# Merged block transfers, units fetched earlier, and head squares moved in a hybrid encoder layer

## The chip, the cores and the metric

One core of one Trainium2 chip runs the whole kernel in one launch. The metric is the device time of an execution in microseconds. TensorE multiplies, VectorE and ScalarE work on tiles, GpSimd masks and gathers, SP only issues transfers, all in program order; they meet at semaphores.

## The reference

One encoder layer over a prompt of 256 tokens and a sample of 1024, together T = 1280 rows of width 1024:

```
xn   = rmsnorm(x, norm1_g)
proj = xn @ w_in                        # pool 512 | q 512 | k 512 | v 512 | o 512 | gates 16
a    = multiscale_pool(proj[pool])      # 4 windows, a 128x128 map for each
m    = sigmoid(o) * head_norm(mlstm_forward(q,k,v) + mlstm_backward(q,k,v)) * head_g
x    = x + concat(a, m) @ w_out
x    = x + hier_moe(rmsnorm(x, norm2_g))   # 32 experts, top 2 in the best group
y    = rmsnorm(x, final_norm_g)
```

The mLSTM has 4 heads of 128 channels and works by chunks of 128 tokens. For a chunk and a direction, with b the running sum of the log forget gates:

```
s    = (q k^T) * exp(logw - m_row)           # logw masked to the direction's triangle
num  = s v + inter * (C q);  den = sum(s) + inter * (n q)
h    = num / max(|den|, exp(-m_row))
C, n = decay * (C, n) + (u * k)^T (v, 1)
```

Then h of both directions is summed, divided by its root mean square per head, and weighted.

## The kernel before

All matrix products with weights are made of three products of a high and a low part (`product3`): `w_hi` is a rounded copy that ScalarE makes, `w_lo` the rest that VectorE makes.

**Projection.** The list `proj` names the input projections, each a slice of 128 output columns by a segment of tokens (512, 512, 256). The last twelve are those of q: four slices of segment 0, four of segment 1, four of segment 2; the last one is NPROJ-1. `w_hi` and `w_lo` hold four slices, `w_st` stages two. A slice m is loaded by `slice_in(m)` on SP, split by `w_part(m)` on ScalarE and VectorE as soon as the slice four before it has been used last. The last four slices, V0 to V3 (NSL-4 to NSL-1), are those of the values; the value projection needs all four and runs over ten token tiles. ScalarE evicts results in `take(n)`, which also splits slices (`parts_after`).

**Blocks.** The parts of the mLSTM that don't depend on the state are made ahead, in 20 blocks of one chunk by two heads (`BLOCKS`): SP loads rows of gate values broadcast to all partitions (`block_in`, two transfers), GpSimd masks, ScalarE takes the exponential (`block_weights`), TensorE transposes keys and makes scores (`block_scores`), VectorE multiplies (`block_products`), SP stores to DRAM (`block_out`, three transfers). Blocks 0 to 7 (N_EARLY) go through three stages beside the last eight q projections, one behind each (`blocks_after`); the others through five stages beside the value projection (`blocks_with`). On SP everything stands in one order: at block i the slices V2 and V3 (i = 4 and 5), then `block_out(i)`, then a `block_in`.

**Scan.** 20 units, a step of one direction each (`unit`): SP loads what the blocks stored (`unit_load`; the first two units into the dead half of `xT_lo`, the others into four slots), TensorE makes numerators and the state's gain (`unit_rows`), VectorE the denominators and the state (`heads_out`), ScalarE evicts h. Beside it the eight slices of w_out come in (`wo_in`) and are split, at each odd unit from 1 to 15. A unit needs the eviction two units before it. As tiles of h are complete in both directions, VectorE sums them (`head_sum`), ScalarE squares them and takes roots (`head_squares`, `head_roots`), VectorE makes the reciprocal, ScalarE scales (`norm_heads`). Six of ten tiles are squared in the scan (EARLY), four behind the first tile of the output projection.

**Output projection.** Ten token tiles (`out_rows`, two halves of 512 columns), each with transposes of h (`h_transposes`), `mix`, its high and low parts, residual, second norm, and the router. Then the expert stage and the final norm.

## Time and profile before

| what | us |
|---|---|
| median of 3 runs | 1243.17 (1243.12 to 1247.94) |
| the profiled execution | 1245.86 |
| its span | 1244.1 |
| TensorE busy | 1115.8 (90%) |
| VectorE busy | 866.1 (70%) |
| ScalarE busy | 683.6 (55%) |
| GpSimd busy | 186.1 (15%) |

Times in the trace are microseconds from the span's start. Projections end at 292, the value projection at 355.8, the scan at 420.2, the output projection at 566; the expert stage takes the rest. Durations of one instruction overlap with those beside it: matmuls are pipelined, so the step from start to start is what counts.

### The profile page before, as it was taken

The numbers are of one execution on the slowest core, as the hardware profiler recorded it, in microseconds if no ns is written. First come the engines' busy times: TensorE is split into PE (matmuls) and PEld (weight loads), VectorE is DVE, ScalarE is ACT, GpSimd is POOL, SyncE is SP. The second block draws the span as 40 slices with busy tenths as digits, with TensorE's granted clock in tenths as the row PEclk, the third lists the DMA queues.
The fourth block names the chain that finished last, engine by engine and source line by source line (L and its number), as shares of the span: only waits on it lengthen the run. The fifth ranks groups of instructions, "written<-read, shape, count | busy, mean of one in ns | idle before, by whom it ended". The sixth has DMA issues, their size and how long they took to land.

```text
span 1244.1 us, 17907 instructions
## 1 busy us (share of the span) xinstructions
PE 1115.8 (90%) x5679; PEld 936.1 (75%) x5679; DVE 866.1 (70%) x1334; ACT 683.6 (55%) x1122; POOL 186.1 (15%) x285
## 2 busy tenths in 40 slices
PE   5999999998988899992799999999999999999910
PEld 4888888887877788882688888888888888888810
DVE  5649510135345566656589999999999999999958
ACT  5432231234346633313577777877877787787633
POOL 1100210001200012223012212211211221221100
PEclk9999999999999999996799999999999999999965
DMA  8212240448988335445889999999999999999667
GB/s 233 60 32 80 89 124 1 120 132 252 298 283 307 134 135 158 148 170 195 282 290 362 384 379 384 370 388 385 380 388 386 384 381 389 376 383 382 251 244 301
DMA packets 161137, 324.04 MB, mean 260 GB/s; under 512 B 24577, under 2 KB 91649, under 8 KB 161089
## 3 DMA queue, kind: packets, MB, share of 16 engines
q1 hardware_dynamic: 145184, 281.81, 63.5%
q0 software_dynamic: 15904, 41.61, 8.7%
q8 instruction: 28, 0.46, 0.1%
q14 instruction: 21, 0.16, 0.0%
HBM read 285.35 MB, written 51.11 MB: 270 GB/s over the span
## 4 chain that ended last, share of the span: by engine, by line
PE 75%; DVE 10%; DMA 5%; ACT 5%; issue 3%; SPq 1%; POOL 1%; ACTq 0%; POOLq 0%; DVEq 0%
PE psum L805 23%; PE psum L807 22%; PE psum L806 22%; DVE e_lo L1718 3%; ACT e_hi L1280 3%; PE psum L1018 2%; PE psum L975 1%; PE psum L1051 1%; DMA w_st<-in_w_out_dram 1%; DVE x L1828 1%; DVE x L1836 1%; DVE x L1826 1%; PE psum L963 1%; PE psum L841 1%; DMA gx<-xn_scratch,rows_to 1%
## 5 line engine op out<-in xcount | busy, mean ns | idle before, releaser
L1718 DVE TENSOR_TENSOR e_lo<-e_st,e_hi 128x1024 fp32r<-128x1024 f32 x384 | 442.6, 1222 | 16.8 <-ACT e_hi L1280 16.0
L1280 ACT ACTIVATE e_hi<-e_st 128x1024 fp32r<-128x1024 f32 x384 | 372.1, 1050 | 10.7 <-PE psum L807 9.8
L805 PE MATMUL psum<-e_hi,ex_hi 128*128 128x512 f32 x512 | 204.8, 400 | 8.6 <-DVE ex_lo L1759 3.7
L806 PE MATMUL psum<-e_lo,ex_hi 128*128 128x512 f32 x512 | 201.3, 393 | 0.0
L807 PE MATMUL psum<-e_hi,ex_lo 128*128 128x512 f32 x512 | 201.1, 393 | 0.0
L805 PE MATMUL psum<-xT_hi,w_hi 128*128 128x512 f32 (+1 forms) x408 | 147.3, 361 | 4.5 <-DVE xT_lo L1399 3.0
L807 PE MATMUL psum<-xT_hi,w_lo 128*128 128x512 f32 (+1 forms) x408 | 145.6, 357 | 0.0
L806 PE MATMUL psum<-xT_lo,w_hi 128*128 128x512 f32 (+1 forms) x408 | 145.5, 357 | 0.0
L805 PEld LDWEIGHTS psum<-e_hi,ex_hi 128*128 128x128 f32 x512 | 96.8, 189 | 41.5 <-DVE e_lo L1718 16.2
L807 PEld LDWEIGHTS psum<-e_hi,ex_lo 128*128 128x128 f32 x512 | 97.0, 189 | 20.9
L806 PEld LDWEIGHTS psum<-e_lo,ex_hi 128*128 128x128 f32 x512 | 97.1, 190 | 19.2
L805 PE MATMUL psum<-e_hi,ht_hi 128*128 128x512 f32 x256 | 105.9, 414 | 1.3 <-DVE yo L1771 1.1
L807 PE MATMUL psum<-e_hi,ht_lo 128*128 128x512 f32 x256 | 100.5, 393 | 0.0
L806 PE MATMUL psum<-e_lo,ht_hi 128*128 128x512 f32 x256 | 100.1, 391 | 0.0
L772 POOL COPY row_to<-rows_to 128x1 int32 (+1 forms) x32 | 28.8, 899 | 417.1 <-DVE yo L1771 417.1
L805 PEld LDWEIGHTS psum<-xT_hi,w_hi 128*128 128x128 f32 x408 | 77.9, 191 | 15.7 <-issue 3.4
L807 PEld LDWEIGHTS psum<-xT_hi,w_lo 128*128 128x128 f32 x408 | 77.8, 191 | 11.0
L1391 DVE TENSOR_TENSOR w_lo<-w_st,w_hi 128x1024 fp32r<-128x1024 f32 x21 | 25.6, 1223 | 86.7 <-ACT w_hi L1088 86.6
L806 PEld LDWEIGHTS psum<-xT_lo,w_hi 128*128 128x128 f32 x408 | 77.8, 191 | 10.7
L805 PE MATMUL psum<-wo_hi,mix_hi 128*128 128x512 f32 x160 | 64.9, 405 | 1.9 <-DVE mix_lo L1624 1.9
L806 PE MATMUL psum<-wo_lo,mix_hi 128*128 128x512 f32 x160 | 63.2, 395 | 0.0
L807 PE MATMUL psum<-wo_hi,mix_lo 128*128 128x512 f32 x160 | 63.1, 394 | 0.0
(226 smaller groups left out, 1717.0 us busy)
## 6 DMA issues: line engine op xcount, KB each, us to landing
e_st<-in_expert_w_gate_dram SPq DMA_DIRECT2D x128, 512.0 KB, 5.6
e_st<-in_expert_w_up_dram SPq DMA_DIRECT2D x128, 512.0 KB, 6.2
e_st<-in_expert_w_down_dram SPq DMA_DIRECT2D x128, 512.0 KB, 8.5
w_st<-in_w_in_dram SPq DMA_DIRECT2D x20, 512.0 KB, 4.2
xn_scratch<-xn POOLq DMA_DIRECT2D x20, 512.0 KB, 3.8
f_y<-expert_rows SPq DMA_DIRECT2D x20, 512.0 KB, 12.2
units<-mlstm_units SPq DMA_DIRECT2D x18, 512.0 KB, 5.4
b_wgt<-gate_rows SPq DMA_DIRECT2D x20, 256.0 KB, 4.5
```

Source lines behind the costliest of these rows:

```text
L772: pool.tensor_copy(row_to[:, b:b + 1], rows_to[:, bass.ds(i, 1)]).then_inc(row_placed, 1)
L805: pe.matmul(out, a_hi, b_hi, start=start, stop=False)
L806: pe.matmul(out, a_hi, b_lo, start=False, stop=False)
L807: return pe.matmul(out, a_lo, b_hi, start=False, stop=stop)
L841: last = pe.matmul(out[:, col:col + m], wpool[:, g, :], u_ext[:, g, first:first + m], start=True, stop=True)
L963: last = pe.transpose(psum[:, 5 + k // 4, (k % 4) * P:(k % 4 + 1) * P], x1[:, order[t], k:D:KD], ident[:, :])
L975: last = pe.matmul(psum[:, 7, 0:NL], x1T[:, k, :], rw[:, k, :], start=(k == 0), stop=(k == KD - 1))
L1018: last = pe.transpose(psum[:, 2 + k // 4, (k % 4) * P:(k % 4 + 1) * P], gx[:, b, k:D:KD], ident[:, :])
L1051: last = pe.transpose(psum[:, 6, k * P:(k + 1) * P], hh[:, k:F:KF], ident[:, :])
L1280: act.activation(e_hi[:, r, :, :], e_st[:, slot, :, :], ACT.Copy).then_inc(ehi_done, 1)
L1391: dve.tensor_tensor(w_lo[:, m % 4, :, :], w_st[:, m % 2, :, :], w_hi[:, m % 4, :, :].bitcast(F32), ALU.subtract).then_inc(wlo_done, 1)
L1718: dve.tensor_tensor(e_lo[:, r, :, :], e_st[:, slot, :, :], e_hi[:, r, :, :].bitcast(F32), ALU.subtract).then_inc(elo_done, 1)
```

## The change

- A block's rows (`rows_dram`), its stage in SBUF and its result in DRAM (`units_dram`) are each laid out in the order weights forward, inter forward, weights back, inter back, keys back. One load and one store do for a block; stage 4 is split over two places and keeps two of each. `back_keys_dram` is gone.
- The blocks 0 and 1 come after the projections NQ+2 and NQ+3 of segment 0, where NQ is now the first q projection, 2 to 5 after those of segment 1, 6 and 7 after NPROJ-3 and NPROJ-1. Blocks 0 and 1 wait for the evictions of the queries of their heads.
- SP issues V2 and V3 at block 7, ahead of `block_out(7)` and behind `block_out(6)`.
- Four units (N_FAR) go to the dead half of `xT_lo`: 0, 1 and 2 are loaded at blocks 11, 13 and 15, unit 3 after the last value projection. A later unit is one transfer in either direction.
- The slices of w_out are split at units 4, 5, 7, 9, 11, 13, 15 and 16 (`wo_at`).
- In the scan ScalarE squares tiles 0 and 1 after units 6 and 8, takes their roots after 10, scales them after 12 and 14, and squares tile 2 after 16; tile 3 follows the scan, and tiles 4 to 9 are squared one at a time in the output projection, with a reciprocal for each. The first tile's transposes, `mix` and `mix_hi` come one unit earlier, `mix_lo` before the last unit.
- The second tile's transposes stand between the fourth and the fifth slice of the first half of the first tile.

```diff
+        wo_at = dict(zip((4, 5, 7, 9, 11, 13, 15, 16), range(KD)))
-        NQ = NPROJ - H * (NS - 1)
+        NQ = NPROJ - H * NS
+        block_at = dict(zip([NQ + 2, NQ + 3] + [NQ + H + c for c in range(H)] + [NPROJ - 3, NPROJ - 1], range(N_EARLY)))
...
             def block_in(i):
-                for kind, dst in ((0, b_wgt[st]), (1, b_qi[st])):
-                    a = 8 * pair + 4 * kind
-                    sp.dma_start(dst[:, :, :, :].rearrange("p d h n -> p (d h) n"),
-                                 rows_dram[a:a + 4, ck * P:(ck + 1) * P].unsqueeze(0)
-                                 .broadcast_to([P, 4, P])).then_inc(blk_in[st], 16)
+                rows = rows_dram[ck, pair, :, :, :]
+                for tile, first, stop in stages[st]:
+                    n = min(stop, 4) - first
+                    sp.dma_start(tile[:, 0:n, :, :].rearrange("p j h n -> p (j h n)"),
+                                 rows[first:first + n, :, :].rearrange("j h n -> (j h n)").unsqueeze(0)
+                                 .broadcast_to([P, n * 2 * P])).then_inc(blk_in[st], 16)
             def block_out(i):
-                for kind, src in ((0, b_wgt[st]), (1, b_qi[st])):
-                    sp.dma_start(units_dram[ck, :, :, kind, heads],
-                                 src[:, :, :, :].rearrange("p d h n -> p d (h n)")).then_inc(blk_out[st], 16)
-                sp.dma_start(back_keys_dram[ck, :, heads],
-                             b_key[st][:, :, :].rearrange("p h n -> p (h n)")).then_inc(blk_out[st], 16)
+                for tile, first, stop in stages[st]:
+                    sp.dma_start(units_dram[ck, pair, :, first:stop, :, :].rearrange("p j h n -> p (j h n)"),
+                                 tile[:, :, :, :].rearrange("p j h n -> p (j h n)")).then_inc(blk_out[st], 16)
...
             for i in range(NB):
-                if i in (N_EARLY // 2, N_EARLY // 2 + 1):
-                    slice_in(NSL - 2 + i - N_EARLY // 2)
+                if i == N_EARLY - 1:
+                    for m in (NSL - 2, NSL - 1):
+                        slice_in(m)
                 block_out(i)
...
-                if i == NB - 4:
-                    sp.wait_ge(proj_ready, NPROJ + 4)
-                    for n in range(2):
+                for n in range(N_FAR - 1):
+                    if i == blocks_with(2 * n + 2)[0]:
+                        sp.wait_ge(proj_ready, NPROJ + 2 * n + 2)
                         unit_load(n)
+            sp.wait_ge(proj_ready, NPROJ + NT)
+            unit_load(N_FAR - 1)
...
-            for n in range(2, 6):
+            for n in range(N_FAR, NU):
                 unit_load(n)
-                if n < 4:
-                    wo_in(n - 2)
-            for n in range(6, NU):
-                unit_load(n)
-                if n % 2 and n // 2 - 1 < KD:
-                    wo_in(n // 2 - 1)
-                if n == 14:
+                if N_FAR + 1 <= n < N_FAR + 3:
+                    wo_in(n - N_FAR - 1)
+                i = wo_at.get(n - 4)
+                if i is not None and 2 + i < KD:
+                    wo_in(2 + i)
+                if n == 13:
...
             def block_scores(i):
                 if i == 0:
                     pe.wait_ge(cols_done, 1)
-                    pe.wait_ge(act_took, act_results(NQ))
+                if i < 2:
+                    pe.wait_ge(act_took, act_results(NQ + 2 * pair + 2))
...
                 unit_rows(n)
-                if n == NU - 2:
+                if n == NU - 3:
                     pe.wait_ge(state_done, states_kept(n))
                     h_transposes(0)
...
-                if t < NT:
-                    out_rows(t, 0)
                 if t == 0:
+                    out_rows(t, 0, 0, 4)
                     pe.wait_ge(h_done, NU)
                     h_transposes(1)
+                    out_rows(t, 0, 4, KD)
+                elif t < NT:
+                    out_rows(t, 0)
...
+                if n == 6:
+                    head_squares(0)
+                elif n == 8:
+                    head_squares(1)
+                elif n == 10:
+                    head_roots(0, 2)
+                elif n in (12, 14):
+                    norm_heads((n - 12) // 2)
+                i = wo_at.get(n)
...
-                if n == NU - 2:
+                if n == NU - 4:
+                    head_squares(2)
+                if n == NU - 3:
                     mix_hi_part(0)
...
-                if t == 0:
-                    for i in range(squared, NT):
-                        head_squares(i)
-                    head_roots(squared, NT)
+                if t + 4 < NT:
+                    head_squares(t + 4)
+                    head_roots(t + 4, t + 5)
```

## Rows read from the trace of the kernel before

**Rows 1.** Windows by stage: us, each engine's busy time, clock, DMA share, GB/s.

```profile
285.50:292.50 7.00, 2.25 (x14) 2.14 (x13) 4.22 (x8) 2.49 (x6) 0.76 (x2) 0.88 0.96 299
292.50:355.80 63.30, 62.55 (x302) 51.89 (x301) 28.11 (x79) 22.27 (x72) 10.73 (x26) 0.99 0.83 261
355.80:420.20 64.40, 50.06 (x420) 47.73 (x420) 39.31 (x133) 40.40 (x138) 0.00 (x0) 1.00 0.76 268
420.20:435.60 15.40, 13.96 (x58) 11.28 (x59) 5.11 (x12) 9.55 (x51) 0.00 (x0) 0.89 0.42 137
435.60:566.00 130.40, 128.55 (x728) 109.35 (x727) 82.82 (x294) 39.18 (x82) 26.45 (x34) 1.00 0.44 150
```

**Rows 2.** Timeline at the turn: start, us, engine, line, operation, idle before.

```profile
252.25 0.60 ACT L1139 ACTIVATE qT<-psum 128x512 f32<-128x512 f32 x1 [4.85 <-PE psum L807]
...
276.77 0.42 DVE L1538 TENSOR_TENSOR kT<-psum,cols 128x256 f32<-128x256 f32 x1
...
277.13 0.60 SPq L469 DMA_DIRECT2D w_st<-in_w_in_dram  x1
...
277.60 0.38 PE L857 MATMUL psum<-ident,kT 128*128 128x128 f32 x2
...
278.08 1.05 ACT L1088 ACTIVATE w_hi<-w_st 128x1024 fp32r<-128x1024 f32 x1
278.10 0.75 DVE L1543 TENSOR_TENSOR b_wgt<-psum,b_wgt 128x256 f32<-128x256 f32 x2
...
290.25 0.44 PE L857 MATMUL psum<-ident,kT 128*128 128x128 f32 x2 [4.75 <-ACT qT L1139]
...
291.18 1.23 DVE L1391 TENSOR_TENSOR w_lo<-w_st,w_hi 128x1024 fp32r<-128x1024 f32 x1 [0.46 <-ACT w_hi L1088]
...
292.46 0.80 PE L805 MATMUL psum<-w_hi,xT_hi 128*128 128x512 f32 x1
```

**Rows 3.** Tile w_st, 215 to 300 us: landing of the w_in slices.

```profile
DMA to landing us min/median/max: 4.0/4.8/6.6
```

**Rows 4.** Timeline, start of the scan, units 0, 1, 2 and 4.

```profile
355.76 0.97 PEld L918 LDWEIGHTS psum<-v,first_units 128*128 128x128 f32 x8 [1.17 <-ACT v L1199]
...
357.65 1.06 PE L918 MATMUL psum<-v,first_units 128*128 128x129 f32 x8
...
361.24 0.49 PE L917 MATMUL psum<-state,units 128*128 128x129 f32 x2 [1.64 <-DMA units<-mlstm_units]
...
366.97 1.16 PE L918 MATMUL psum<-v,units 128*128 128x129 f32 x8 [0.43 <-DMA units<-mlstm_units]
```

**Rows 5.** Windows, two microseconds of the scan with full DMA.

```profile
372.00:374.00 2.00, 1.72 (x15) 1.75 (x16) 0.64 (x2) 1.24 (x5) 0.00 (x0) 1.00 1.03 419
```

**Rows 6.** Timeline, middle of the scan: two wo_lo in turn, units 14 and 15.

```profile
384.79 1.23 DVE L1633 TENSOR_TENSOR wo_lo<-w_st,wo_hi 128x1024 fp32r<-128x1024 f32 x1 [4.01 <-ACT wo_hi L1252]
...
390.14 1.23 DVE L1633 TENSOR_TENSOR wo_lo<-w_st,wo_hi 128x1024 fp32r<-128x1024 f32 x1 [1.14 <-ACT wo_hi L1252]
...
400.51 0.39 PE L917 MATMUL psum<-state,units 128*128 128x129 f32 x2
...
403.19 0.39 PE L917 MATMUL psum<-state,units 128*128 128x129 f32 x2
```

**Rows 7.** Groups by line and tile h_fb: table load, squares.

```profile
L1212 ACT ACT_TABLE_LOAD x1 | 1.3, 1283 | 0.0
...
L1206 ACT ACTIVATE h_fb<-h_fb x40: 293/294/312, 378.7 to 434.7; 128x128 f32<-128x128 f32 x40
```

**Rows 8.** Timeline, first tile of the output projection.

```profile
420.26 0.58 PE L805 MATMUL psum<-wo_hi,mix_hi 128*128 128x512 f32 x1 [1.87 <-DVE mix_lo L1624]
...
427.43 0.60 PE L933 MATMUL psum<-ident,h_fb 128*128 128x128 f32 x4
...
429.41 0.63 PE L933 MATMUL psum<-ident,h_fb 128*128 128x128 f32 x4 [1.38 <-DVE mixf L1616]
```

**Rows 9.** Tile w_st, 355 to 412 us: landing of the w_out slices.

```profile
DMA to landing us min/median/max: 5.4/6.4/7.4
```

More of the change, by code:

```diff
@@ L152, in build, with stage_part @@
     ROWS2 = ROWS + 5 * KB
-    stages = [(V0, V0 + 2 * KB, V0 + 4 * KB), (ROWS, ROWS + 2 * KB, ROWS + 4 * KB),
-              (ROWS2, ROWS2 + 2 * KB, ROWS2 + 4 * KB), (W_ST, W_ST + 2 * KB, W_ST + 4 * KB),
-              (V0 + 5 * KB, W_ST + 5 * KB, V0 + 7 * KB)]
-    b_wgt = [at(f"b_wgt{i}", o[0], [P, 2, 2, P], F32) for i, o in enumerate(stages)]
-    b_qi = [at(f"b_qi{i}", o[1], [P, 2, 2, P], F32) for i, o in enumerate(stages)]
-    b_key = [at(f"b_key{i}", o[2], [P, 2, P], F32) for i, o in enumerate(stages)]
+    WGT_F, QI_F, WGT_B, QI_B, KEY_B = range(5)
+    stages = [[(at(f"stage{i}", off, [P, 5, 2, P], F32), 0, 5)] for i, off in enumerate((V0, ROWS, ROWS2, W_ST))]
+    stages.append([(at("stage4a", V0 + 5 * KB, [P, 3, 2, P], F32), 0, 3), (at("stage4b", W_ST + 5 * KB, [P, 2, 2, P], F32), 3, 5)])
+    def stage_part(st, j):
+        tile, first, _ = next(x for x in stages[st] if x[1] <= j < x[2])
+        return tile[:, j - first, :, :]
+    N_FAR = 4
     first_units = at("first_units", X0 + 40 * KB, [P, KD, T], F32)
-    units = [at(f"units{i}", Q0 + 6 * KB * i if i < 3 else V0, [P, 3 * H, P], F32) for i in range(4)]
+    units = [at(f"units{i}", Q0 + 6 * KB * i if i < 3 else V0, [P, H // 2, 6, P], F32) for i in range(4)]
     def unit_part(n, j):
-        if n < 2:
-            t = 2 * n + j // 6
-            return first_units[:, j % 6, t * P:(t + 1) * P]
-        return units[(n - 2) % 4][:, j, :]
+        pair, idx = j % H // 2, 2 * (j // H) + j % 2
+        if n < N_FAR:
+            t = 2 * n + pair
+            return first_units[:, idx, t * P:(t + 1) * P]
+        return units[(n - N_FAR) % 4][:, pair, idx, :]
     c_off = [Q0]
@@ L415, in stage_of, with stage_signals @@
             return i % 3 if i < N_EARLY else (i - N_EARLY) % 5
-        def stage_uses(i):
-            return sum(stage_of(j) == stage_of(i) for j in range(i))
+        def stage_signals(st, upto):
+            return 16 * len(stages[st]) * sum(stage_of(j) == st for j in range(upto))
         def wait(eng, s, value):
@@ L547, in unit_load @@
+                parts = 2 * (stop - first)
+                src = units_dram[ck, :, :, first:stop, :, :].rearrange("b p j h n -> p b (j h) n")
+                if n < N_FAR:
+                    for pair in range(H // 2):
+                        t = 2 * n + pair
+                        sp.dma_start(first_units[:, 0:parts, t * P:(t + 1) * P], src[:, pair, :, :]).then_inc(arrived, 16)
                     return
-                slot = units[(n - 2) % 4]
-                sp.dma_start(slot[:, 0:2 * H, :], src).then_inc(arrived, 16)
@@ L550, in unit_load @@
-                if d:
-                    sp.dma_start(slot[:, 2 * H:3 * H, :], keys).then_inc(arrived, 16)
+                sp.dma_start(units[(n - N_FAR) % 4][:, :, 0:parts, :], src).then_inc(arrived, 16)
             def wo_in(i):
@@ L946, in out_rows @@
             def out_rows(t, half, first=0, stop=KD):
-                if half == 0:
+                if half == 0 and first == 0:
                     pe.wait_ge(mixlo_done, t + 1)
@@ L1248, in _ @@
                 ins.then_inc(h_done, 1)
-                if n % 2 and n // 2 < KD:
-                    i = n // 2
+                if n == 6:
[7 more added lines that the diff above has]
+                i = wo_at.get(n)
+                if i is not None:
                     act.wait_ge(wo_load[i % 2], 16 * (i // 2 + 1))
@@ L1629, in _ @@
                 heads_out(n)
-                if n % 2 and n // 2 < KD:
-                    i = n // 2
+                if n == NU - 3:
+                    mix(0)
+                if n == NU - 2:
+                    mix_lo_part(0)
+                i = wo_at.get(n)
+                if i is not None:
                     dve.wait_ge(wohi_done, i + 1)
@@ L1721, in _ @@
             dve.wait_ge(consts_done, N_CONST)
-            head_reciprocal(2, 2, EARLY)
+            for i in (2, 3):
+                head_reciprocal(i, i, i + 1)
             for t in range(NT + 1):
```

93 lines of the change are left out of this document (36 added, 57 removed).

## The prediction

> **What bounds the kernel now.** I read the windows by stage first. TensorE sets the pace nearly everywhere: in the value projection (292.5 to 355.8 us) it is busy 62.6 of 63.3 us and in the output projection (435.6 to 566) 128.6 of 130.4. Nothing that the change puts there can gain, and the expert stage behind it is not touched. Three stretches are left [rows 1]. At the turn from query to value projection, 285.5 to 292.5, TensorE is busy 2.3 of 7.0 us. In the scan over the 20 units, 355.8 to 420.2, it is busy 50.1 of 64.4. In the first tile of the output projection, 420.2 to 435.6, it is busy 14.0 of 15.4 at a mean clock of 0.89. These hold 4.8 + 14.3 + 1.4 = 20.5 us of idle time, and the low clock of the last one costs about 15.4 x 0.11 = 1.7 us more. The timelines of these stretches come second, since a wait must be seen with what is queued before it; the tiles' landing times third.
>
> **Part 1: one run per partition for the blocks.** A block's two broadcast loads become one (4 KB runs for 512 B), its three stores one (5 KB runs for 1 KB); the last of the five stages keeps two of each, being split over two tiles. Same bytes, fewer descriptors, about three issues less on SP per block. Who waits? In the value projection nobody on the path: TensorE has only 0.8 us of idle time there [rows 1]. At the turn, before: block_scores(8) waits for the eviction of the last query projection, which sits on ScalarE behind the exponentials of block 6, whose rows landed late; TensorE stood 4.75 us [rows 2]. The loads of that block are what part 1 and the new places of the early blocks bring forward: blocks 2 to 5 now follow the four 512-column projections, and block 7 is loaded some 9 us before its use.
>
> **But the two last value slices move too.** SP issued them before block_out(4) and block_out(5), the first at 277.13 [rows 2]. Now both stand behind block_out(6), which waits for the products of block 6, and block 6 comes after the last but two projection. Step by step: that projection ended at 277.60 with five blocks done. Six are done now, one more at 0.58 us (my reading of the step from one projection to the next, an estimate), and block 1 waits for the eviction of the very projection that TensorE has just issued: ScalarE starts some 0.2 us after the projection's end and takes 0.60 for 512 columns [rows 2], with the signal 0.87 (an estimate). So it ends at 277.60 + 0.58 + 0.87 = 279.05. ScalarE's w_hi of slice V1 starts 0.48 later and takes 1.05 (277.60, 278.08 [rows 2]), so 280.6; VectorE's w_lo (1.23 [rows 2]) ends at 281.9; the products of block 6 take from 276.77 to 278.85, 2.1 us [rows 2], so 284.0; the store is issued, and V2 at 284.7, V3 at 285.3. Landing is 4.0 to 6.6, median 4.8 [rows 3]: 289.5. Only then does ScalarE split V2 (1.05), evict the last query projection (0.36), split V3 (1.05), and VectorE makes w_lo of V3 (1.23): 293.3, where the first value projection begins. It began at 292.46 [rows 2]. So the wait keeps its size and changes its cause, from the rows of a block to a weight slice: **+0.8 us**, with bounds 0 (landing 4.0) and +2.6 (landing 6.6).
>
> **Part 2: four units fetched beside the value projection.** The scan starts at 355.76; units 0 and 1 were there, unit 2 waited 1.64 us for its transfer, and unit 4 started at 366.97, again on a transfer [rows 4]. Now units 0 to 2 land under the projection, where the DMA share is 0.83 [rows 1] and the blocks' transfers get cheaper; nobody waits there. Unit 3 is issued after the last value projection (355.6) and has until unit 2 ends. The waiting loads hold up SP's queue with block_out and block_in behind them, but the value projections they wait for are done by then: cost zero while SP keeps up with one block in 6.2 us, of which it used 2.8 for issues. Units 0 to 3 then take 1.9 us each, as 355.76 to 357.65 did: with the 0.8 from the turn, 356.6 + 4 x 1.87 = 364.0 for unit 4. That is **3.0 us** earlier than 366.97. Behind it stand 0.5 + 0.8 + 0.5 + 0.5 + 0.5 + 0.8 MB of units 4 to 7 and two slices of w_out, issued from 357.1 on; at 0.4 MB/us (419 GB/s in a full window [rows 5]) they land by 361 to 369, before TensorE asks (364 to 371).
>
> **Part 3: the scan from unit 4 on.** What is late next is a chain over two engines. Undisturbed, a unit takes 403.19 - 400.51 = 2.68 us on TensorE, and a pair of units with one slice of w_out takes 390.14 - 384.79 = 5.35 us from wo_lo to wo_lo [rows 6]: 1.23 (wo_lo), 0.5 (denominators), 1.1 (eviction of the even unit), 1.1 (of the odd one), 1.07 (wo_hi), that is all of the 5.36 that TensorE has. Any other work of ScalarE between the two evictions comes on top. The change puts one such piece into each pair: squares of a tile after units 6 and 8, roots with their table load after 10, norms after 12 and 14. Squares of a tile are 4 x 0.30 us (0.294 at one start after the other [rows 7]), so 1.2; norms the same; roots 1.28 for the table [rows 7] and 0.3. As VectorE covers 0.3 of it, a pair takes 6.3 us. With the two slices after units 4 and 5 the chain reaches the end of wo_lo(1) at 373.1, and five pairs of 6.3, 0.3 more for the roots and 0.5 for the first sums bring the end of wo_lo(6) to 405.4. Then wo_hi(7), wo_lo(7), two sums, squares of tile 2, the denominators of unit 17, mix(0), mix_hi and mix_lo of tile 0 follow one another: 10.3 us of such durations, so the output projection starts at **415.8**, 4.4 us before its 420.26 [rows 8]. TensorE alone could be there by 406; the gap is the rival below. Against the 3.0 at unit 4 this is only 1.4 more: three squares fewer before the scan's end (3.6 us) are mostly paid back by the piece in every pair.
>
> **Part 4: first tile of the output projection.** Transposes of the second tile (427.43) came after the whole half, and those of the third then waited 1.38 us for mix(1) [rows 8]. Now they stand in the middle, and mix(1) runs under the second four slices: **-1.4 us**. The squares of six tiles go to ScalarE at one tile per 12.9 us, 1.2 us each with a root of 0.3, beside 39 of 130 us busy [rows 1]: nothing. The six small reciprocals on VectorE (83 of 130 busy) stand behind the routing, before the next residual: 0 to 0.3 us each if that was on the path, which 128.6 of 130.4 us of TensorE deny. What is late next is TensorE itself.
>
> **Sum.** -4.4 (which holds the +0.8 and the -3.0) - 1.4 = -5.8 us. The profiled execution took 1245.86 us, 1244.1 of it span, 2.7 above the median of the three runs; the difference is taken from the median: 1243.17 - 5.8 = **1237.4 us**.
>
> **A page against a row.** While the scan runs, TensorE is busy 78% in bursts with gaps up to 2.7 us, and its granted clock is 1.00 [rows 1]; it fell to 1.2 GHz only after the 4.75 us at the turn (mean 0.88) and at the start of the output projection (0.89). The Trainium skill, page "TensorE: Matmul & The Clock Gate", section "HAM oscillation", says that a kernel whose bursts are separated by waits is throttled anew after each one that is long enough. By that rule gaps of the new scan would matter as well as the turn; the trace agrees for the long wait and not for the short ones, so the sum keeps both low stretches where they are.
>
> **Rivals.**
> A, *the pieces on ScalarE don't add up*: VectorE and ScalarE have more play than my chain gives, pairs take 5.5 us. Then wo_lo(6) ends 4 us sooner and the gain is about 10: 1233.5. For: the same kinds of pieces stood in the scan before, and with all the waits for transfers they left TensorE only 14.3 us idle [rows 1]. Against: the chain of 5.35 has no slack. 0.25.
> B, *the turn is cured*: the slices land before ScalarE asks. Then 4.75 us of wait and some 1.5 us of low clock go too: another 6, 1231.5. Against: the first is issued 7.6 us later than before. 0.06.
> C, *the clock moves*: in the new tail unit 18, a wait of 2.9 us, unit 19 and another wait follow one another. If the clock falls there already, unit 19 and the first half of the tile run at 1.2 GHz: +2 us, 1239.5. If it does not fall at all: -1.7. This is of the size of the first and stays in the range. By the page named above the fall would come; 0.12 for it.
> D, *slower*: SP's queue. Each wo_in now waits for the wo_lo two slices before it and the unit loads stand behind it; wo_in(4), for one, holds the load of unit 12 until 380. It lands at 385 for a use at 388, and unit 14, behind the mixer loads, lands at 395.4 for a use at 395.1. w_out slices land in 5.4 to 7.4 us [rows 9]. From about 8 us per landing on, units 9, 12, 14, 16 and 18 each wait 2 to 3 us: +13, 1250. Against: the DMA is less full than before after 400. 0.06.
> E, *nothing changes* at the end of the scan, because VectorE's chain through wo_lo(7), the sums and mix(0) was the same length before: only the 3 us at unit 4 remain, 1240.2. 0.16.
> The forecast itself: 0.35.
>
> **From the cases.** About 0.5% (6.2 us, to 1237.0) is what a measurement of this kernel can tell from no change, and my forecast lies next to that line. A, B and two fifths of the forecast's cases lie beyond it: 0.25 + 0.06 + 0.14 = 0.45 faster. Slower by 6.2: D and little of C, 0.07. The rest, 0.48, is within. The range leaves out D and the ends of B: from 1230.5 (A with landings of 4.0 and no low clock) to 1244 (E with +2.6 at the turn and the clock).
>
> **What would show it.** Right: in the timeline the first value projection at 293 +- 1, with block_scores(8) waiting some 4 us for the qT eviction and ScalarE before that for w_st; unit 4 at 364; wo_lo to wo_lo 6.3 us; output projection from 416. Wrong: unit 4 not before 366 (then unit 3's transfer is late), TensorE waits on transfers of units beyond 5, pairs of 5.4, or an output projection in which TensorE idles.

## The result, and the profile after

| | us |
|---|---|
| before, median of 8 runs | 1245.69 (1243.12 to 1248.2) |
| after, median of 8 runs | 1238.66 (1235.91 to 1240.53) |
| ratio | 0.9939, 95% interval 0.9925 to 0.9952 |
| profiled execution after, its span | 1236.62, 1234.9 |
| predicted | 1237.4 (1230.5 to 1244.0) |

The kernel is faster by 0.61% (the ratio, 7.6 us of 1245.69), or 7.0 us by the medians. The forecast was a gain of 5.8 us, taken from a median of three runs that five more raised by 2.5. So the hit in absolute time (1.3 us off) is partly luck, and the difference is the better measure: 1.2 us more gain than forecast. The two profiled executions lie 9.2 us apart, one of each kernel: the one before is close to its median, the one after 2.0 us below its own. What follows is read from them, with that in mind.

The windows by stage after the change, to be laid beside [rows 1] (same stretches, same columns: busy time of TensorE, its weight loads, VectorE, ScalarE, GpSimd, then the clock, the DMA share and GB/s):

```profile
285.50:292.50 7.00, 2.64 (x16) 2.45 (x15) 2.07 (x2) 3.26 (x7) 0.00 (x0) 0.84 0.66 184
292.50:355.80 63.30, 62.55 (x305) 51.95 (x304) 28.26 (x80) 20.88 (x70) 9.46 (x24) 0.99 0.76 264
355.80:420.20 64.40, 56.69 (x444) 54.29 (x445) 43.31 (x142) 41.36 (x138) 0.00 (x0) 0.95 0.75 269
420.20:435.60 15.40, 15.40 (x78) 12.92 (x77) 6.25 (x10) 7.69 (x27) 1.10 (x2) 1.00 0.65 223
```

The turn is as idle as it was (2.64 us busy of 7.0, 2.25 before). TensorE's busy time in the value projection is the same to the hundredth. Nearly all of the gain is in the third and fourth rows: TensorE does 6.6 us more work before 420.2, and the first tile of the output projection has no idle time. The DMA share of the value projection fell from 0.83 to 0.76 although three units are fetched there where it was two, and a fourth at its end. In the whole execution 161137 packets became 135808 for the same 324.04 MB, so part 1 made the transfers cheaper; nobody on the path waited for them there.

The turn, timeline after (start, us, engine, line, operation, idle before), against [rows 2]:

```profile
283.68 0.32 SPq L533 DMA_DIRECT2D mlstm_units<-stage  x1
...
284.04 1.81 SPq L474 DMA_DIRECT2D w_st<-in_w_in_dram  x2
...
289.08 1.06 ACT L1094 ACTIVATE w_hi<-w_st 128x1024 fp32r<-128x1024 f32 x1 [6.10 <-DMA w_st<-in_w_in_dram]
290.04 0.37 ACT L1145 ACTIVATE qT<-psum 128x256 f32<-128x256 f32 x1
...
290.46 0.69 PE L861 MATMUL psum<-ident,kT 128*128 128x128 f32 x2 [4.36 <-ACT qT L1145]
```

Both slices leave SP right behind the store of block 6 at 283.68. ScalarE idles 6.10 us for the first of them, the query eviction stands behind its split, and block_scores(8) waits 4.36 us for that eviction. The wait has its old size (4.75 [rows 2]) and the new cause that the prediction named. The first value projection starts at 292.94.

The scan, TensorE's timeline: the scan's start, unit 4, unit 14 and unit 19, then the output projection:

```profile
355.79 1.16 PE L922 MATMUL psum<-v,first_units 128*128 128x129 f32 x8 [0.75 <-ACT v L1205]
...
363.30 1.13 PE L922 MATMUL psum<-v,units 128*128 128x129 f32 x8
...
394.31 0.49 PE L921 MATMUL psum<-state,units 128*128 128x129 f32 x2 [2.01 <-DMA units<-mlstm_units]
...
410.49 0.77 PE L921 MATMUL psum<-state,units 128*128 128x129 f32 x2 [2.90 <-ACT h_fb L1241]
...
413.92 0.78 PE L808 MATMUL psum<-wo_hi,mix_hi 128*128 128x512 f32 x1
```

Unit 4 starts with no wait, 3.67 us earlier than in [rows 4]. The output projection starts 6.34 us earlier than in [rows 8]. Between them lie two long waits: 2.01 us for the transfer of unit 14, and 2.90 us for an eviction ahead of unit 19.

What paces the middle is seen in VectorE's timeline, in the wo_lo of slices 1 to 4:

```profile
371.05 1.23 DVE L1641 TENSOR_TENSOR wo_lo<-w_st,wo_hi 128x1024 fp32r<-128x1024 f32 x1 [1.57 <-ACT wo_hi L1256]
...
377.68 1.22 DVE L1641 TENSOR_TENSOR wo_lo<-w_st,wo_hi 128x1024 fp32r<-128x1024 f32 x1 [1.22 <-ACT wo_hi L1256]
...
383.72 1.22 DVE L1641 TENSOR_TENSOR wo_lo<-w_st,wo_hi 128x1024 fp32r<-128x1024 f32 x1 [1.83 <-ACT wo_hi L1256]
...
390.22 1.22 DVE L1641 TENSOR_TENSOR wo_lo<-w_st,wo_hi 128x1024 fp32r<-128x1024 f32 x1 [2.29 <-ACT wo_hi L1256]
```

Steps of 6.63, 6.04 and 6.50; the next two are 6.11 and 6.04, a mean of 6.26 for a forecast of 6.3, where a pair without a piece on ScalarE took 5.35 [rows 6]. VectorE waits for wo_hi each time. The chain of waits says the same (start, us, what). This is one pair, the one with the roots and their table load:

```profile
385.46 1.14 ACT h_fb L1241 x4
386.62 1.28 ACT L1218
387.91 0.30 ACT hstat L1218
388.21 1.03 ACT h_fb L1241 x4
389.24 0.95 ACT wo_hi L1256
390.25 1.11 issue
```

Eviction, table load (1.28) and root (0.30), eviction, wo_hi: the chain runs through ScalarE and no longer through TensorE. The idle 2.01 us for unit 14 isn't on it: the chain goes past TensorE there. The end of the chain, ahead of the output projection:

```profile
407.37 0.70 DVE h_fb L1608
408.09 1.11 ACT h_fb L1212 x7
409.27 1.12 ACT h_fb L1241 x4
410.49 0.77 PE psum L921 x2
```

and the granted clock around it (windows, columns as above):

```profile
408.00:410.00 2.00, 0.00 (x0) 0.00 (x0) 1.93 (x9) 1.91 (x11) 0.00 (x0) 0.93 0.00 0
410.00:414.00 4.00, 3.52 (x17) 3.54 (x17) 3.29 (x10) 2.47 (x7) 0.00 (x0) 0.50 0.01 2
414.00:417.00 3.00, 3.00 (x10) 2.39 (x9) 2.90 (x8) 1.74 (x9) 0.00 (x0) 0.57 0.00 0
```

TensorE works at 1.2 GHz from unit 19 to about 416.5, then at 2.4 GHz again (1.00 from 417 to 420). From the start of the output projection to the first residual it takes 13.41 us (413.92 to 427.33), where it took 15.33 (420.26 to 435.59).

### The profile page after: what moved, and what is told of

Read it like the earlier page. It is cut to its first block, busy times and chain, and to the rows that moved or that the text cites. A ratio compares the mean times of both kernels' runs of the same rounds, so it can differ in the third digit from the quotient of the medians.

```text
span 1234.9 us, 17854 instructions
## 1 busy us (share of the span) xinstructions
PE 1113.7 (90%) x5679; PEld 935.0 (76%) x5679; DVE 866.8 (70%) x1340; ACT 684.6 (55%) x1128; POOL 185.3 (15%) x285
## 2 busy tenths in 40 slices
DMA packets 135808, 324.04 MB, mean 262 GB/s; under 512 B 23552, under 2 KB 60320, under 8 KB 135760
## 4 chain that ended last, share of the span: by engine, by line
PE 78%; DVE 9%; ACT 6%; DMA 3%; issue 3%; POOL 0%; ACTq 0%; SPq 0%; POOLq 0%; DVEq 0%
PE psum L808 23%; PE psum L810 22%; PE psum L809 22%; DVE e_lo L1723 3%; ACT e_hi L1284 3%; PE psum L1024 2%; PE psum L979 1%; PE psum L1057 1%; ACT h_fb L1241 1%; DVE x L1834 1%; DVE x L1842 1%; PE psum L922 1%; DVE x L1832 1%; PE psum L863 1%; PE psum L967 1%
## 6 DMA issues: line engine op xcount, KB each, us to landing
f_y<-expert_rows SPq DMA_DIRECT2D x20, 512.0 KB, 12.1
```

## The experiments

Each is an edit of the kernel after. Ratios are against the kernel before, run beside the experiment on the same chip; the kernel after has 0.9939 (0.9925 to 0.9952) from runs of its own. The medians of the kernel before were 1245.46 beside e1 to e4, 1245.71 beside e5, e8, e9 and e10, and 1246.88 beside e7 and e11, so medians of two experiments can be compared to a microsecond at best. The profiled executions reach the same point ahead of the turn up to 3.5 us apart (block_scores(6) starts at 278.87 in the kernel after, at 279.04 in e8, at 280.47 in e9 and at 282.37 in e7), whatever the edit, so stages are compared by their lengths. The four points that I use, in us of each trace (e1 and so on as labelled below):

| | first value projection | scan | output projection | first residual | median |
|---|---|---|---|---|---|
| before | 292.46 | 355.76 | 420.26 | 435.59 | 1245.69 |
| after | 292.94 | 355.79 | 413.92 | 427.33 | 1238.66 |
| e1 | 289.18 | 351.70 | 410.91 | 423.71 | 1232.46 |
| e2 | 293.40 | 356.70 | 413.89 | 426.42 | 1236.42 |
| e3 | 289.11 | 351.63 | 408.63 | 420.82 | 1233.22 |
| e4 | 294.08 | 357.84 | 419.04 | 431.47 | 1240.06 |
| e5 | 293.77 | 357.42 | 415.51 | 429.26 | 1238.73 |
| e7 | 291.68 | 354.23 | 409.43 | 421.58 | 1230.40 |
| e8 | 288.29 | 350.82 | 405.52 | 417.65 | 1228.28 |
| e9 | 295.03 | 358.33 | 416.36 | 428.52 | 1239.82 |
| e10 | 294.09 | 359.13 | 419.17 | 431.57 | 1241.32 |
| e11 | 294.21 | 357.89 | 415.79 | 428.12 | 1238.30 |

**e1, the slices one block earlier.** Is it the two slices behind block_out(6) that hold the turn?

```
-                if i == N_EARLY - 1:
+                if i == N_EARLY - 2:
                     for m in (NSL - 2, NSL - 1):
                         slice_in(m)
```

> The changed kernel with the value slices V2 and V3 issued one block earlier on SP, ahead of block_out(6) instead of behind it. My theory (the wait at the turn is now that of a weight slice held up in SP's queue): V2 is issued near 279 and V3 near 282 instead of 284.0 and 284.6, ScalarE doesn't wait for them, TensorE's wait before block 8 falls from 4.4 us to under 1.5, the clock stays at 1.00 there, and the kernel gains 4 to 6 us on the changed one (ratio to the kernel before 0.989 to 0.991 instead of 0.9939). Rival (the wait is that of blocks, or given back in the value projection by block rows that land later): the wait keeps 4 us or moves behind the first value projections; ratio 0.993 to 0.995.

Measured: 1232.46 us (5 runs), ratio 0.9897 (0.9882 to 0.9912). The slices leave at 279.86, and the 4.36 us wait is gone; 0.66 for w_lo is left. Issue and first value projection of e1, and then the window 286 to 296 of the kernel after and of e1:

```profile
279.86 3.43 SPq L474 DMA_DIRECT2D w_st<-in_w_in_dram  x2
...
289.18 0.50 PE L808 MATMUL psum<-w_hi,xT_hi 128*128 128x512 f32 x1 [0.66 <-DVE w_lo L1395]
```

```profile
286.00:296.00 10.00, 5.64 (x25) 5.06 (x25) 4.81 (x9) 3.56 (x7) 0.00 (x0) 0.83 0.45 128
```

```profile
286.00:296.00 10.00, 9.34 (x56) 8.05 (x55) 3.85 (x9) 2.49 (x6) 0.00 (x0) 1.00 0.50 189
```

TensorE is busy 9.34 of 10 us for 5.64, at a clock of 1.00 for 0.83. The intervals of e1 and of the kernel after don't touch: the place of two DMA issues in SP's list costs 5 to 6 us. This settles the cause of the wait at the turn. From the start of block_scores(6) to the first value projection it takes 9.25 us, the kernel after 14.07. Not all of that arrives in this trace: the scan takes 59.2 us for 58.1, since after the wait at unit 14 the clock fell here and not in the kernel after.

**e2, the pieces on ScalarE behind wo_hi.** Does the piece between the two evictions of a pair set its 6.3 us?

```
-                if n == 6:
-                    head_squares(0)
...
                                    ACT.Copy).then_inc(wohi_done, 1)
+                if n == 7:
+                    head_squares(0)
+                elif n == 9:
+                    head_squares(1)
+                elif n == 11:
+                    head_roots(0, 2)
+                elif n in (13, 15):
+                    norm_heads((n - 13) // 2)
...
-                if n == 11:
+                if n == 12:
                     head_reciprocal(1, 0, 2)
```

> The changed kernel with ScalarE's pieces in the scan (squares of tiles 0 and 1, their roots, their norms) moved from behind the even units 6 to 14, between the two evictions of a pair, to behind the split of w_out at the odd units 7 to 15, where ScalarE stands idle while VectorE makes wo_lo. The reciprocal of the two tiles goes one unit later. My theory (the scan is bound by the chain over ScalarE and VectorE, with the piece in it): a pair takes 5.4 to 5.6 us from wo_lo to wo_lo instead of 6.0 to 6.6, and the kernel gains 3 to 4 us on the changed one (ratio 0.990 to 0.992). Rival (the transfers of the units, behind the mixer loads, or TensorE's own order bind as well): the pieces leave the chain, but TensorE waits for units 12 to 14 instead; gain under 1.5 us (ratio 0.993).

Measured: 1236.42 us (6 runs), ratio 0.9926 (0.9908 to 0.9945). VectorE's timeline of e2, slices 2 to 6 of w_out, and TensorE at unit 14:

```profile
378.52 1.22 DVE L1641 TENSOR_TENSOR wo_lo<-w_st,wo_hi 128x1024 fp32r<-128x1024 f32 x1 [1.14 <-ACT wo_hi L1248]
...
383.88 1.23 DVE L1641 TENSOR_TENSOR wo_lo<-w_st,wo_hi 128x1024 fp32r<-128x1024 f32 x1 [1.14 <-ACT wo_hi L1248]
...
389.23 1.23 DVE L1641 TENSOR_TENSOR wo_lo<-w_st,wo_hi 128x1024 fp32r<-128x1024 f32 x1 [0.96 <-ACT wo_hi L1248]
...
394.65 1.22 DVE L1641 TENSOR_TENSOR wo_lo<-w_st,wo_hi 128x1024 fp32r<-128x1024 f32 x1 [1.02 <-ACT wo_hi L1248]
...
402.58 1.23 DVE L1641 TENSOR_TENSOR wo_lo<-w_st,wo_hi 128x1024 fp32r<-128x1024 f32 x1 [0.71 <-ACT wo_hi L1248]
```

```profile
395.08 0.49 PE L921 MATMUL psum<-state,units 128*128 128x129 f32 x2 [2.62 <-DMA units<-mlstm_units]
```

Pairs of 5.36, 5.35 and 5.42: the mechanism is shown, the piece was all of the difference. Then one pair of 7.93: TensorE comes to unit 14 sooner and waits 2.62 us for its transfer, and this time the wait is on the path. The scan gets shorter by 0.9 us only (57.2 for 58.1). In time the gain can't be told from none, as the intervals overlap widely; the 3 to 4 us that I expected did not come, the rival did. The transfer of unit 14 was hidden right behind the chain over ScalarE.

**e3, both edits.**

> Both edits of the two runs before together: V2 and V3 one block earlier and ScalarE's pieces behind the odd units. If the two waits are independent, as my theory has it, the gains add up: 7 to 10 us on the changed kernel (ratio 0.986 to 0.988). Rival: with an earlier start of the scan the same transfers and the slices of w_out come later against it, and less than 5 us remain (ratio 0.990).

Measured: 1233.22 us (5 runs), ratio 0.9902 (0.9884 to 0.9919), not to be told from e1 alone; the 7 to 10 us of both together did not come. Its trace has both effects, the first value projection at 289.11 and pairs of 5.35 to 5.42, and again a wait of 2.25 us at unit 14, and 2.41 at unit 19. From first value projection to first residual it takes 131.7 us, e1 134.5, the kernel after 134.4. That gain of 2.8 us in the trace doesn't show in the medians; the profiled execution is the fastest of the five (1230.95).

**e4, unit 2 fetched behind the value projection.** One of the four units of part 2 is moved back.

```
-                for n in range(N_FAR - 1):
+                for n in range(N_FAR - 2):
...
             sp.wait_ge(proj_ready, NPROJ + NT)
+            unit_load(N_FAR - 2)
             unit_load(N_FAR - 1)
```

> The changed kernel with unit 2 loaded after the last value projection together with unit 3, so that only two units are there when the scan starts, as before the change. My theory (fetching ahead brought 3 of the microseconds): TensorE waits about 1.5 us for unit 2 and up to 2 for unit 3, unit 4 starts 2 to 4 us later, and since the chain over ScalarE takes over only from unit 7 on, nearly all of it arrives at the end: 2 to 3.5 us lost (ratio 0.996 to 0.997). Rival (the chain over the two engines has the slack to swallow it): under 1 us lost (ratio 0.994).

Measured: 1240.06 us (6 runs), ratio 0.9956 (0.9939 to 0.9973). TensorE's waits in e4:

```profile
363.98 0.49 PE L922 MATMUL psum<-state,first_units 128*128 128x129 f32 x2 [0.51 <-DMA first_units<-mlstm_units]
...
398.59 0.49 PE L922 MATMUL psum<-state,units 128*128 128x129 f32 x2 [3.41 <-DMA units<-mlstm_units]
```

Unit 2 itself does not wait; unit 3, whose transfer now stands behind it, waits 0.51 us. Unit 4 starts 8.0 us after the scan's start for 7.5, and from the first wo_lo on the chain runs some 0.8 us late. The wait at unit 14, thirty us later, grows from 2.01 to 3.41, and there the clock falls (0.64 from 398 to 402). The scan takes 61.2 us instead of 58.1. By the medians the loss is 1.4 us, with overlapping intervals: the direction is as expected, its size in time isn't settled. The likely reading is that a transfer issued later pushes back all that stand behind it in a stretch where the DMA is full (share 1.03 from 398 to 402). No run separates this from the low clock, which makes up a part of the 3.1 us.

**e5, the transposes of the second tile behind the whole first half, as before.**

```
-                    out_rows(t, 0, 0, 4)
+                    out_rows(t, 0)
                     pe.wait_ge(h_done, NU)
                     h_transposes(1)
-                    out_rows(t, 0, 4, KD)
```

> The changed kernel with the second tile's transposes put back behind the whole first half of the first tile. My theory: TensorE waits again for mix(1) before the third tile's transposes, 1.2 to 1.4 us, with nothing else moved: ratio 0.995 instead of 0.9939. Rival (with tile 3's squares now ahead of it on ScalarE, the norm of tile 2 is late as well, or the wait was covered): no difference, 0.994.

Measured: 1238.73 us (5 runs), ratio 0.9937 (0.9924 to 0.9951), the same as the kernel after. In its trace the old wait is back:

```profile
423.12 0.63 PE L937 MATMUL psum<-ident,h_fb 128*128 128x128 f32 x4 [1.39 <-DVE mixf L1619]
```

From output projection to first residual it takes 13.75 us, the kernel after 13.41, but the two have different shares of the low clock: in e5 it ended 0.1 us into the stretch, in the kernel after 2.6 us. What it costs is half of the time for which it lasts, 0.06 and 1.32 us. Without it the stretch takes 13.69 us in e5 and 12.09 in the kernel after; by the same account it takes 12.13 to 12.19 in e1, e2, e3, e4, e7, e8, e9 and e11, which all have the transposes in the new place (12.40 in e10, which also has other squares beside it). So the traces show part 4 at 1.5 us. The medians can't: 1.5 us is 0.12% against intervals of 0.27%.

**e9, the block transfers split again** (two loads and three stores for each, as before; the blocks keep their new places).

```
-                for tile, first, stop in stages[st]:
-                    n = min(stop, 4) - first
+                for tile, off, first, stop in pieces(st, 4):
+                    n = stop - first
...
-                for tile, first, stop in stages[st]:
+                for tile, off, first, stop in pieces(st, 5):
...
+            cut = [(max(a, first), min(b, stop), tile, first) for tile, first, stop in stages[st]
+                   for a, b in ((0, 2), (2, 4), (4, 5)) if b <= end and max(a, first) < min(b, stop)]
```

> The changed kernel with each block's one load made in two transfers (of 2 KB a partition) and its one store in three (2, 2 and 1 KB a partition), so as many transfers as before the change, all else as changed. My theory (the merging is off the path): SP has 3 more issues per block, blocks land up to 1 us later, V2 is issued about 1 us later at the turn because two more issues of block_out(6) stand before it, and that is all: 0.5 to 1.5 us lost, ratio 0.9945 to 0.995. Rival (the merging is what carries the gain, by transfers that land sooner): 3 us or more lost, with waits of TensorE inside the value projection, ratio 0.9965 or more.

Measured: 1239.82 us (5 runs), ratio 0.9953 (0.994 to 0.9967). At the turn block_scores(8) waits 4.71 us instead of 4.36, and the first value projection starts at 295.03, 2.1 us later; 1.6 of it arose ahead of the turn, and from the start of block_scores(6) it is 14.56 us for 14.07. Behind it no wait comes back. By the medians the split costs 1.2 us, with overlapping intervals. What the trace shows of it is 0.5 us at the turn, in the one place where a store's issue stands ahead of a slice that TensorE will wait for. The run has 144448 packets, not the 161137 of the kernel before, since the rows stay in their new order in DRAM: it tests the number of transfers, and the larger descriptors only in part.

**e10, the head squares back in the scan** (tiles 2 to 5 in units 17 and 19, the last four behind the first tile of the output projection).

```
+                if n in (17, 19):
+                    head_squares(n - 15)
+                    head_squares(n - 14)
                 act.wait_ge(rdn_done, n + 1)
...
-                if n == NU - 4:
-                    head_squares(2)
...
-            head_squares(3)
...
+                if t == 0:
+                    for i in range(6, NT):
+                        head_squares(i)
                 if t + 4 < NT:
-                    head_squares(t + 4)
```

> The changed kernel with the squares put back about where they were: tiles 2 and 3 ahead of unit 17's eviction, tiles 4 and 5 ahead of unit 19's, tiles 6 to 9 together behind the first tile. My theory: at the end of the scan every piece ahead of an eviction is on the chain: 1.2 us more before unit 19, and 2.4 us before the last eviction, of which the transposes of the second tile wait for a part; the four at once stand beside TensorE's work as before. 1 to 2.5 us lost (ratio 0.995 to 0.996). Rival (moving the squares gained nothing): ratio 0.994.

Measured: 1241.32 us (5 runs), ratio 0.9961 (0.9947 to 0.9974). The wait ahead of unit 19 grows to 3.56 us (2.90), the scan takes 60.0 us (58.1). Half of the 1.9 us stands at the scan's end: from the start of wo_lo(7) to the output projection it takes 8.64 us for 7.69. The other half arose at unit 14, where the clock fell in this execution (0.57 from 398 to 402) and the pair took 6.98 us for 6.04, ahead of all the squares that were moved. So this part carries 1.0 us by the trace and 2.7 by the medians, whose intervals overlap a little.

**e8, a faster version.** e3 with two more edits, against what was left: the four mixer loads (1 MB), which stand in SP's list ahead of unit 14, go behind unit 16; and the squares of the third tile go behind unit 18, out of the way of the eviction that unit 19 waits for.

```
-                if n == 13:
+                if n == 16:
                     sp.wait_ge(hss_done, 2)
                     for i in range(2):
                         mixer_in(i)
...
-                if n == NU - 4:
+                if n == NU - 2:
                     head_squares(2)
```

> Both edits (value slices one block earlier, ScalarE's pieces behind the odd units), and two more: the loads of pooled values and gates for the first two tiles go from unit 13 to unit 16 on SP, so that unit 14's load doesn't stand behind them, and the squares of tile 2 go from behind unit 16 to behind unit 18. My theory: the wait of 2.25 us for unit 14's transfer and most of the 2.4 us before unit 19 go, the output projection starts near 404 instead of 408.6, and the kernel gains 3 to 5 us on both edits alone (ratio 0.985 to 0.988). Rival (TensorE's wait is only handed on to the next link, mix(0) and its parts on VectorE and ScalarE): the output projection starts after 407 and the ratio stays at 0.990.

Measured: 1228.28 us (1226.58 to 1228.51, 5 runs), ratio 0.9852 (0.9839 to 0.9866): 1.5% below the kernel before and 0.9% below the kernel after. TensorE's waits at the end of the scan, and a window over them:

```profile
395.76 0.49 PE L921 MATMUL psum<-state,units 128*128 128x129 f32 x2 [1.14 <-DMA units<-mlstm_units]
...
402.26 0.46 PE L921 MATMUL psum<-state,units 128*128 128x129 f32 x2 [1.32 <-ACT h_fb L1241]
...
405.52 0.47 PE L808 MATMUL psum<-wo_hi,mix_hi 128*128 128x512 f32 x1 [1.24 <-DVE mix_lo L1628]
```

```profile
398.00:406.00 8.00, 5.44 (x45) 5.06 (x44) 7.14 (x20) 4.12 (x17) 0.00 (x0) 1.00 0.12 48
```

The wait at unit 14 is gone (the pair is 5.35 there too). Three short waits, for the transfer of unit 17, for the eviction ahead of unit 19 and for mix_lo, stand where one long one was, and the clock stays at 1.00. In the kernel after the mixer loads hold unit 14's load back on SP as well, from 385.37 to 388.62 (SP's list):

```profile
385.37 1.50 SPq L562 DMA_DIRECT2D mixf<-pooledT  x1
...
388.62 1.84 SPq L550 DMA_DIRECT2D units<-mlstm_units  x2
```

Which of the two edits did it? The next two runs take them apart.

**e7, e3 with the mixer loads moved, the squares not.**

> Both edits of the run with slices and pieces moved, and the two mixer loads issued at unit 16 of SP's list instead of 13, squares of the third tile left behind unit 16. This takes the run with the squares moved as well apart. Theory (the mixer loads in front of unit 14's load were the cost): unit 14's wait of 2.25 us is gone, the sixth wo_lo to the seventh is 5.4 us and not 7.6, wo_lo(6) starts near 394 instead of 397.15, and the output projection starts near 405.5 instead of 408.6. TensorE still waits 2.4 us for unit 19 and unit 19 runs at 1.2 GHz. Time 3 us below the run with both edits: 1230. Rival (the squares were the gain): the transfer wait moves to unit 17 or 18 at its full size, the output projection starts at 407.5 or later, and the time stays at 1232.5 to 1233.5; the step to 1228.3 then came from the clock at unit 19.

Measured: 1230.4 us (1227.7 to 1230.92, 5 runs), ratio 0.9864 (0.9844 to 0.9884), not to be told from e8. TensorE's waits in e7:

```profile
399.66 0.49 PE L921 MATMUL psum<-state,units 128*128 128x129 f32 x2 [1.60 <-DMA units<-mlstm_units]
...
406.23 0.46 PE L921 MATMUL psum<-state,units 128*128 128x129 f32 x2 [1.40 <-ACT h_fb L1241]
...
409.43 0.47 PE L808 MATMUL psum<-wo_hi,mix_hi 128*128 128x512 f32 x1 [1.18 <-DVE mix_lo L1628]
```

The scan takes 55.2 us (57.0 in e3, 54.7 in e8), and the median is 2.8 us below e3, though the intervals of their ratios just meet (at 0.9884). So the mixer loads were the cost; whether by their bytes or by their time in SP's list no run tells. My expectation that unit 19 would still wait 2.4 us at 1.2 GHz was wrong: TensorE comes there later, after a wait for the transfer of unit 17 (1.60 us), and the idle time is split.

**e11, the kernel after with the squares moved alone.**

> The changed kernel with one edit: the squares of the third tile stand behind unit 18's eviction instead of unit 16's, so the eviction that unit 19 waits for comes 1.1 us earlier. Theory (it is the 2.9 us wait there that brings the clock down): unit 19 starts after a wait of 1.8 us, the clock stays at 1.00 from 408 to 420, unit 19 takes 1.9 us instead of 3.4, and TensorE waits instead some 1.2 us for mix_lo, so the output projection starts within 0.3 us of 413.9 (counted from the scan's start 58.1 us) but its first tile is at full clock: 0.7 to 1.3 us below the changed kernel, 1237.6. Rival (the tail is VectorE's chain, and the clock costs nothing because it falls under that chain): the start is the same and the time is the same within 0.4 us, 1238.7. If the clock falls nevertheless, the wait's length is not what decided it.

Measured: 1238.3 us (6 runs), ratio 0.9933 (0.9914 to 0.9951), the same as the kernel after. My theory falls, the rival holds. VectorE's and ScalarE's timeline of e11 ahead of unit 19:

```profile
408.34 1.23 DVE L1641 TENSOR_TENSOR wo_lo<-w_st,wo_hi 128x1024 fp32r<-128x1024 f32 x1 [1.14 <-ACT wo_hi L1256]
409.48 1.29 DVE L1608 TENSOR_TENSOR h_fb<-h_fb 128x512 f32<-128x512 f32 x2
410.69 0.15 DVE L1587 TENSOR_TENSOR dn<-psum,cols 128x4 f32<-128x4 f32 x1
...
411.28 1.14 ACT L1241 ACTIVATE h_fb<-psum,rdn 128x128 f32<-128x128 f32 x4 [2.98 <-DVE rdn L1590]
```

With the squares out of the way ScalarE waits 2.98 us for the denominators, which stand on VectorE behind wo_lo(7) and two sums. In the kernel after the same squares filled that wait. The tail is VectorE's: from the start of wo_lo(7) to the output projection it takes 7.45 us in e7, e8 and e11 alike, 7.69 in the kernel after.

## Why the prediction was right, and where it was off

**The turn.** Right in cause, order and size: slices issued at 284.04 (284.7 foretold), landing 5.0 us later (4.8), first value projection 292.94 (293.3). One thing was left out: the low clock ended sooner. Of the value projection 1.7 us lay in it before and 0.7 us now. So the value projection took 62.85 us, 0.45 less than before, and the scan started at 355.79, level with before, and the +0.8 came to nothing. e1 prices this stall, rival B, at 5 to 6 us, as the prediction said (6): it is the largest loss that the change left.

**Unit 4** started 3.67 us earlier for a forecast of 3.0, the difference being just that scan start. Of units 5 to 13 only unit 7 may have waited for its transfer: TensorE stood 0.38 us ahead of it, and in e1 and e11 the trace names the DMA there.

**The chain of two engines.** Right: pairs of 6.26 on average for 6.3, and e2 shows by pairs of 5.35 that the pieces on ScalarE are the difference. Rival A (pairs of 5.5) and rival E (the same length at the end, a gain of 3 us only) didn't come. One sum in it is loose: the five steps of an undisturbed pair were said to fill the 5.36 us, but 1.23, 0.5, 1.1, 1.1 and 1.07 make 5.0. The measured 5.35 was what the forecast used, so nothing hangs on it. The term that was mis-sized stands in the step from the end of wo_lo(1) to the end of wo_lo(6): the five pairs took 31.3 us, and I had added 0.3 for the roots and 0.5 for sums to 31.5. The pair with the roots took 6.50, but others took 6.04 to 6.11. With the 0.8 of the start this makes the end of wo_lo(6) 403.6 instead of 405.4. From there 10.3 us to the output projection, measured 10.3: 413.92 for 415.8. So the gain there was 6.3 us, not 4.4.

**The first tile** gained 1.9 us (15.33 to 13.41), where -1.4 stood. The wait of 1.38 is gone; the clock is the other part, and here rival C had its sign wrong. It did fall at unit 19, as that rival said. But unit 19 at 1.2 GHz costs nothing there, or 0.4 us at most, since the output projection needs mix_lo, which VectorE finishes at 413.5, a little before TensorE is through:

```profile
412.31 1.22 DVE L1628 TENSOR_TENSOR mix_lo<-mixf,mix_hi 128x1024 fp32r<-128x1024 f32 x1 [0.64 <-ACT mix_hi L1235]
```

So part of the low clock is spent under VectorE's chain, and the clock was back to 1.00 by 417, only 3 us into the tile; before it was low for most of 420 to 424. With half of its low stretch taken off, the tile took 13.62 us before (e5, with the transposes in the old place, 13.69) and takes 12.09 now: 1.5 us of the gain are the transposes, 0.4 us the clock (1.71 us lost before, 1.32 now). Where the clock was full throughout, in e7, e8 and e9, the tile took 12.1 to 12.2 us.

**Rival D**, late transfers of units, was half right. Unit 14 waited 2.01 us, near the place that it named (394.31, for 395.4 foretold), and the prediction's list had "TensorE waits on transfers of units beyond 5" as a sign of being wrong. It cost nothing, because the chain over ScalarE passed there at the same time. e2, e4 and e3 show it as soon as the cover goes, and e7 shows its cause, the 1 MB of mixer loads ahead of it (an estimate of their time is 2.5 us, at the 413 GB/s measured from 394 to 398).

**The sum.** -6.3 and -1.9 make -8.3 at the first residual, for -5.8 forecast; the medians say -7.0 with an interval of 6.0 to 9.3 (0.9952 and 0.9925 of 1245.69). Of the 9.2 us between the spans of the two profiled executions 0.9 arises behind the first tile; no run was made for that.

**The clock against the page.** The Trainium skill, page "TensorE: Matmul & The Clock Gate", section "HAM oscillation", says that waits of sufficient length between bursts bring the throttle back. The rows agree that waits bring it down, and show that the wait's length alone does not decide: after 2.62 us of wait at unit 14 in e2 the clock stayed at 1.00 (395 to 399), after 2.40 us at unit 19 of the same run it fell (0.70 from 410 to 413), and TensorE had been busy without a gap for 4 us ahead of either. After shorter waits at unit 14 it fell in e1 and in e10:

```profile
390.46 0.49 PE L921 MATMUL psum<-state,units 128*128 128x129 f32 x2 [2.23 <-DVE state L1600]
```

```profile
397.53 0.49 PE L921 MATMUL psum<-state,units 128*128 128x129 f32 x2 [1.88 <-DMA units<-mlstm_units]
```

The clock was 0.57 from 391.5 to 395.5 in e1 and from 398 to 402 in e10. No run here tells what decides. Rival C took the page to say that the clock would fall at its wait of 2.9 us; the section speaks of waits that are long enough and doesn't say that this one is.

## What to carry to other kernels

When stores and loads share one in-order issue queue, look at what a moved store now holds up: two weight loads behind a store that waits for a computation cost 5 to 6 us here, several times the 1.2 us, inside the intervals, that splitting the block transfers again cost. When two engines hand a tile back and forth, count what each does between its two turns and put side work in the slack behind the hand-over, not between; then ask at once which transfer was hidden behind the old pace, since here most of the gain was lost to it until that one was moved too. A wait of TensorE that the chain does not pass through costs nothing now and can be the first bill when the chain is shortened, as unit 14's was.

## What the hardware showed that was not expected

- Waits of nearly the same length had different effects on the clock. At the end of the scan e7 and e8 have waits of 1.1 to 1.6 us and keep the clock at 1.00; the kernel after and all its other edits have one of 2.4 to 3.6 us ahead of unit 19, and the clock falls to 1.2 GHz. But the kernel before lost it there behind waits of 0.78 and 1.87 us (0.57 from 420 to 424), and at unit 14 it fell after 1.88 us in e10 and stayed after 2.62 us in e2.
- A low clock costs only what the path sees of it: unit 19 took 3.4 us at 1.2 GHz in the kernel after (410.49 to 413.92) under a chain of VectorE that was no shorter.
- 161137 DMA packets became 135808 for the same 324.04 MB, and the DMA share of the value projection fell from 0.83 to 0.76, while that stage took 63.30 us before and 62.85 after, a difference that the clock's earlier rise makes up (see the turn above). With the transfers split again (e9) it is 144448 packets and 1.2 us more in the medians, less than the intervals can tell. No run has the old packets of 512 B with all else as changed, so what the larger descriptors alone are worth stays open; in the stage where the share fell hardly anybody waited for them.
